# Expert one's up matrix in one transfer, with no wait for the first row fetch ahead of expert two's planes

## The reference, cut to what matters

```
def expert_block(args):
    xb, e = args
    a = jnp.dot(xb, w_gate[e])      # 1024 x 512, float32: 2 MiB
    u = jnp.dot(xb, w_up[e])        # 2 MiB
    return jnp.dot(jax.nn.silu(a) * u, w_down[e])   # 512 x 1024: 2 MiB
```

## Time and profile before

| | us |
|---|---|
| median of 3 runs | 1014.39 |
| lowest, highest | 1013.24, 1016.46 |
| the profiled execution, its own time | 1014.47 |
| its span, first to last instruction | 1012.7 |
| TensorE busy | 912.2 (90%) |
| DMA queue q1, share of 16 engines over the span | 65.6% |
| chain that ended last: TensorE, DMA | 65%, 27% |
| of it: transfers of up matrices | 25% |

### The profile page before, as it was taken

One profiled execution on the slowest core, in us unless ns is written; L12 is line 12 of the kernel. 1 busy time (PEld: TensorE's weight loads), 2 busy tenths in 40 slices (PEclk: granted clock), 3 DMA queues, 4 the chain that ended last, 5 costly groups with the idle time before them and its releaser, 6 DMA issues.

```text
span 1012.7 us, 16250 instructions
## 1 busy us (share of the span) xinstructions
PE 912.2 (90%) x6727; PEld 659.8 (65%) x6730; DVE 380.8 (38%) x984; ACT 258.6 (26%) x525; POOL 143.2 (14%) x149
## 2 busy tenths in 40 slices
PE   8999999989999999998999999877778777877996
PEld 7969995457999997986444554534444334434775
DVE  4279998754333355353111111101011010013796
ACT  6354328664231242230000000000000000002542
POOL 2705432122110000000111111110110101001000
PEclk9999999999999999997999999999999999998998
DMA  9860602005734406489999999999999999996701
GB/s 269 96 161 1 208 2 63 1 2 148 221 96 105 126 1 271 155 330 372 419 428 426 426 427 425 426 427 426 427 424 428 426 428 427 425 413 261 301 22 67
DMA packets 60764, 265.99 MB, mean 263 GB/s; under 512 B 11152, under 2 KB 36128, under 8 KB 46592
## 3 DMA queue, kind: packets, MB, share of 16 engines
q1 hardware_dynamic: 54784, 253.22, 65.6%
q0 software_dynamic: 5296, 9.71, 2.6%
q10 hardware_dynamic: 624, 2.23, 0.6%
HBM read 256.22 MB, written 16.85 MB: 270 GB/s over the span
## 4 chain that ended last, share of the span: by engine, by line
PE 65%; DMA 27%; DVE 4%; ACT 2%; issue 2%; SPq 0%; DVEq 0%; ACTq 0%; POOLq 0%
DMA arena<-in_w_up 25%; PE ps L1247 14%; PE ps L1429 12%; PE ps L1447 5%; PE ps L1102 5%; PE ps L1280 4%; PE ps L1564 4%; PE ps L1048 3%; PE ps L1023 2%; PE ps L1192 2%; PE ps L1171 1%; PE ps L1537 1%; PE ps L1141 1%; PE ps L1342 1%; PE ps L985 1%
## 5 line engine op out<-in xcount | busy, mean ns | idle before, releaser
L1429 PE MATMUL ps<-arena,hT 128*64 128x256 f32 x2048 | 245.2, 393 | 39.4 <-DMA arena<-in_w_up 19.6
L1429 PEld LDWEIGHTS ps<-arena,hT 128*64 128x64 f32 x2048 | 148.7, 136 | 145.6 <-DMA arena<-in_w_up 28.0
L2401 DVE TENSOR_TENSOR xf<-xf,ps 128x256 f32<-128x256 f32 x32 | 13.5, 422 | 384.5 <-PE ps L1429 384.5
L1247 PE MATMUL ps<-arena_merge,arena_merge 128*128 128x256 f32 x624 | 99.7, 287 | 0.0
L1861 ACT ACTIVATE xf<-ps 128x512 f32<-128x512 f32 x32 | 19.1, 597 | 302.8 <-PE ps L1447 302.8
L929 POOL DMA_INDIRECT expert_rows<-xf,arena x32 | 32.8, 1023 | 409.0 <-ACT xf L1861 409.0
L1247 PEld LDWEIGHTS ps<-arena_merge,arena_merge 128*128 128x128 f32 x624 | 87.4, 188 | 0.0
L1447 PE MATMUL ps<-arena,xf 128*64 128x512 f32 x328 | 75.0, 597 | 13.8 <-DVE xf L2404 11.9
L1247 PE MATMUL ps<-xf_merge,arena_merge 128*128 128x256 f32 x480 | 82.1, 288 | 0.0
L1247 PEld LDWEIGHTS ps<-xf_merge,arena_merge 128*128 128x128 f32 x480 | 69.2, 188 | 0.2 <-DVE arena_merge L2206 0.2
L1447 PEld LDWEIGHTS ps<-arena,xf 128*64 128x64 f32 x328 | 24.2, 136 | 50.6 <-issue 37.7
(11 more groups left out here) (333 smaller groups left out, 1302.7 us busy)
## 6 DMA issues: line engine op xcount, KB each, us to landing
arena<-in_w_gate SPq DMA_DIRECT2D x31, 2048.0 KB
arena<-in_w_up SPq DMA_DIRECT2D x30, 2048.0 KB, 39.1
arena<-in_w_down SPq DMA_DIRECT2D x10, 2048.0 KB, 41.3
arena<-in_w_down SPq DMA_DIRECT2D x20, 1024.0 KB
hT<-in_w_down SPq DMA_DIRECT2D x10, 2048.0 KB
arena<-in_w_in SPq DMA_DIRECT2D x10, 1024.0 KB, 6.6
arena<-in_w_in SPq DMA_DIRECT2D x3, 2048.0 KB, 11.3
arena<-in_w_ple_gate SPq DMA_DIRECT2D x2, 2048.0 KB, 14.0
```

The source lines that it names most:

```text
L1247: mm = pe.matmul(w[:, 2 * lo_t:lo_t + hi_t], rounded(st[:, c, cols]), rounded(mv[:, c, lo_t:hi_t]), start=c == 0 and k == 0, stop=c == pla ...
L1429: mm = pe.matmul(ps[g * BLK:(g + 1) * BLK, 2 + m, s * 256:(s + 1) * 256], xsT[:, c, s * BLK:(s + 1) * BLK], expert_columns(k, slice(m, m + ...
```

## The change

The wait for the first gather's landing between the halves of expert 1's up matrix goes, and with it the split: the matrix is loaded by one transfer of eight planes, and expert 2's planes are issued right behind it. `FIRST_LOADS` counts one transfer instead of two.

```diff
-FIRST_LOADS = ((1, 1, 2), (1, 2, 4))
+FIRST_LOADS = ((1, 1, 2), (1, 1, 4))
...
         load_planes(1, 0, 0, KD)
         sp.wait_ge(part_used, 2)
         sp.wait_ge(rows_full, TILES)
-        load_planes(1, 1, 0, KD // 2)
-        sp.wait_ge(xs_in[0], 16)
-        load_planes(1, 1, KD // 2, KD)
+        load_planes(1, 1, 0, KD)
         load_planes(2, 1, 5, 8)
         load_planes(2, 0, 2, KD)
         load_planes(2, 1, 0, 1)
         load_planes(2, 1, 3, 5)
```

## The result

Over six runs of each on one chip the changed kernel takes 1018.48 us at the median (1017.17 to 1020.62), the kernel before 1015.33 (1013.11 to 1016.90). The ratio, taken of the means, is 1.0037, 95% interval 1.0021 to 1.0053: slower by 3.8 us, between 2.1 and 5.4. The profiled execution took 1018.08 us with a span of 1016.3, 3.6 more than before on both counts. The forecast was + 2.8 us; the measured medians differ by 3.2, the means by 3.8.

The account below looks back on a forecast made before the run. DMA bytes bound the kernel: an unbroken weight stream from about 475 us. Its beginning 2.2 us later plus 0.6 for a slow start, 2.8 on 1014.47, gave 1017.3 us; range for 8 in 10: 1013.9 to 1020.2.

Parts of the forecast that it names:

- What sets the end: Experts: the end is the beginning of an unbroken weight stream, from about 475 us, plus its bytes over 427 GB/s.
- What the removed hold gives: DMA engines in 457 to 461: 2.35 us of stream regained, of which at most 0.6 us can reach the end.
- The gather's burst: First gather's packets sharing the engines with a full q1: 5.7 us from 454.7, where it took 2.9.
- the store's share of it: ScalarE's store of the last tile beside the first gather: some 7 packets of 4 KB on an engine, 1.1 us.
- The gather's landing: First gather, ahead of TensorE's first rows: lands 2.8 us later, at about 460.9.
- Packet for packet: Queue sharing on each engine: a packet of q0 waits for about one packet of q1, whatever its size.
- The prediction's case by that rule: First gather passing in one turn: delayed by one turn of q1, nothing to 3.1 us; sum 1014.5 to 1017.6.
- From the gather to the gate matmuls: TensorE behind the landing: no gap swallows a delay, so all 2.8 us reach the gate matmuls.
- The clock: TensorE's half-clock stretches in 457.8 to 464.5 and 468 to 471.4: 1.2 us either way, set at 0.
- The stream's beginning: Stream at expert 3's gate matrix: begins at 477.5 instead of 475.3, + 2.2 us; with the slow start 2.8.
- The backlog lost: Queue ahead of expert 3's gate matrix: only 0.6 us of backlog, and dry after the change.
- the slow start: Transfer of expert 3's gate matrix on an idle queue: slow at first, charged 0.6 us (0 to 0.75).

Follow-up runs that it names:

- e7: The changed kernel with ScalarE's store of the last tile held until the first gather has landed; ratio to the kernel before 1.0047.
- e2: The changed kernel with expert 1's up matrix and expert 2's planes there in transfers of one or two planes; ratio to the kernel before 1.0029.
- e3: The changed kernel with the wait for the gather put behind the whole up matrix, ahead of expert 2's planes; ratio to the kernel before 1.0037.
- e1: The kernel before with only the wait for the first gather taken out, the up matrix still in two halves; ratio to the kernel before 1.0037.
- e4: The changed kernel with the wait for the gather put ahead of the whole up matrix and planes; ratio to the kernel before 0.9998.
- e12: e4 with six idle matmuls of TensorE between the gather's landing and the first rows; ratio to the kernel before 1.0023.
- e8: The kernel before with six up planes issued by GpSimd behind the gather on its queue, the rest held until the landing; 1014.16 us, ratio 1.0000.
- e10: The kernel before with two planes of expert 1's up matrix ahead of the hold and six behind it; ratio to the kernel before 1.0007.

## Why the prediction was right, step by step

**What sets the end** held. The shape of the chain is the same, each link of an up matrix moved by 3.1 to 3.2 us. In the table, the kernels that issue expert 3's gate matrix earlier than 22 us after the gather gain 1 us at most for a lead of up to 4.4 us; those that issue it 0.8 to 3.0 us later lose 1.3 to 4.4 us (last up matrix). By their runs the first four do not differ from before, and all the others are slower.

**What the removed hold gives** held: nothing shows at the end. The dip is filled, and 4.5 us of standstill stand instead ahead of the down row, which waits for TensorE.

**The gather's burst** held to 0.2 us (5.9 measured, 5.7 forecast), and so did the store's share of it (0.8 to 0.9 us by e7, 1.1 forecast). Its terms held less well: forecast were 81 packets of 16 KiB and 3.9 turns of 6 KiB, nine turns in all on an engine; of the 182 packets of q1 that passed, 11.4 for each engine, 133 are under 8 KB. The burst began later, and more of the up matrix had gone by then. With e2 and e3, where the same sum failed by length or by count, the good total is partly luck. **The gather's landing** was mis-sized: 4.4 us late, 2.8 forecast. The term left out is the wait for the first turn. I let the burst begin at 454.7 as before; but in the changed kernel no packet of q0 moves in 452 to 456.6:

```profile
q1 hardware_dynamic: 103, 1.44, 91.3%
q8 instruction: 1, 0.02, 1.4%
```

The kernel before in the stretch that ends at 454.7 (450 to 454.7, the same columns); the earlier trace rows hold the gather whole:

```profile
q1 hardware_dynamic: 151, 1.49, 88.5%
q8 instruction: 1, 0.02, 1.2%
```

So the first packet comes 4.6 us from the issue, where it was 3.0 before. These 1.6 us are the difference between forecast and landing. Packet for packet, the reason for the 5.7, is roughly right where q1's pieces are of 6 KiB and more (changed kernel, e1) and wrong for 2 and 4 KiB (e2).

By the Trainium skill ("DMA: Bandwidth & Descriptors", section "Queues, rings and completion order") an engine drains a whole packet of some 9 to 17 descriptors from one queue before it goes to the next. The prediction's case by that rule had a delay of at most 3.1 us; it was 4.4, and the gather's 144 packets did not pass in one turn but over 5.9 us, beside 182 of q1.

**From the gather to the gate matmuls** held to the letter: 4.64 us late at the first rows, 4.59 at the gate matmuls.

**The clock**, set at 0 with 1.2 us either way, gave back 1.35 us, a little beyond that range. Before, TensorE ran at 0.50 in 457.8 to 464.5 and again in 468 to 471.4, which fell on the gate matmuls. In the changed kernel it stands at 0.50 in 458.3 to 468.6, the longer idle time and the first rows in it, and is full when the gate matmuls begin. The 64 gate and up matmuls take 7.47 us, in e4 and e12 as well, where the clock stood at 1.00 from 455 until they were done; where it was granted 0.60 and 0.58 at their beginning, in e8 and e10, they took 8.76 and 8.94. So 4.6 us of lateness became 3.24 at expert 3's gate matrix, where 2.8 had been forecast.

**The stream's beginning**: 3.24 us became 3.12 at the last up matrix. The backlog lost (0.6) and the slow start (0.6) were to cancel. Their sum came out as forecast; neither has been measured by itself.

So the forecast was right in sign and in its mechanism, and near in size by luck: two errors of 1.6 and 1.35 us took each other away. The first runs of the kernel before had a median 0.94 us lower than all six together, which is why 1018.5 lies 1.2 us above the forecast time while the difference is off by 0.4 (by 1.0 if means are taken). The result lies just beyond the border of 0.3% on the slow side, with an interval that reaches under it; I had given that side 0.42 and the other 0.54, so the likelier of the two by my own chances did not come.

## What to carry to other kernels

A hold that leaves DMA engines idle need not be a loss. Here the held traffic would have delayed the work that releases the next loads, and the queue ran empty ahead of them with the hold and without. To see it, count the bytes between the idle time and the next load that waits for compute, and see whether the queue is empty there. A small transfer that compute waits for pays for the bulk traffic let out around it: here 1 MB of it cost 2.8 us, 5 MB 7.2. To know which of two resources sets an end, delay one of them alone and leave the other as it is.

## What had not been expected of the hardware

The wait of an indirect transfer for its first packet depends on the bulk queue: 1.8 us after issue with nothing let out (e4), 3.0 with 1.05 MB, 4.4 with 2.1 MB (e3), 4.6 with 5.2 MB. It does not simply follow the backlog: with 0.52 MB (e10) it was 1.8 too, while q1 was 89% busy until then, and between 2.1 and 5.2 MB it hardly grows. What holds back the first packet has not been tried apart, and stays open. Smaller pieces in the bulk queue (2 and 4 KiB in place of 6 and 8) did not let the gather through any sooner, 9.84 us against 9.78.
